# Moving the chunk inverses and the selection against each other in a two-block transformer kernel

## The reference

```python
# DeltaNet branch: a scan over chunks, after a triangular inverse for each chunk
lmat = jnp.where(strict, jnp.einsum('nbhid,nbhjd->nbhij', k_beta, kc) * decay, 0.0)
tmat = lax.linalg.triangular_solve(eye + lmat, eye, left_side=True, lower=True, unit_diagonal=True)
u = jnp.einsum('nbhij,nbhjd->nbhid', tmat, v_beta)
w = jnp.einsum('nbhij,nbhjd->nbhid', tmat, k_beta * jnp.exp(gc)[..., None])
# per chunk: v_new = u - w @ state ; o = q @ state + a @ v_new ; state = decay * state + k^T @ v_new

# Sparse attention branch: an index score picks the keys
dots = jnp.einsum('bqhd,bsd->bqhs', qi_b, ki)
score = jnp.einsum('bqh,bqhs->bqs', wi_b, jax.nn.relu(dots))
score = jnp.where(causal[None], score, -jnp.inf)
_, idx = lax.top_k(score, 128)      # for each block of 128 queries
```

## Time and profile before

| | us |
|---|---|
| median of 3 runs (1946.12 to 1949.91) | 1947.81 |
| the profiled execution's own time | 1946.41 |
| its span, first to last instruction | 1944.6 |
| TensorE busy | 1930.8 (99%) |
| VectorE busy | 1018.0 (52%) |
| ScalarE busy | 888.2 (46%) |
| GpSimd busy | 850.2 (44%) |

### The profile page before, as it was taken

How to read it: one execution, slowest core, us unless ns; L and a number is a source line. 1 busy time by engine, 2 the same in 40 slices (tenths; PEclk the granted TensorE clock), 3 DMA queues, 4 the chain that set the end, 5 groups by cost and what they waited for, 6 DMA issues and landing times.

```text
span 1944.6 us, 23731 instructions
## 1 busy us (share of the span) xinstructions
PE 1930.8 (99%) x9106; PEld 1532.8 (79%) x9106; DVE 1018.0 (52%) x1832; ACT 888.2 (46%) x1355; POOL 850.2 (44%) x644
## 2 busy tenths in 40 slices
PE   9999999999999999999999999999999999999999
PEld 6878887877788878787877888677766788888887
DVE  5757755555745668766464647575644436101210
ACT  6455553344345455543344355586555344312321
POOL 5545432433445454422434445455322445444443
PEclk9999999999999999999999999999999999999999
DMA  5334542423535235632414545322111332222232
GB/s 202 128 118 131 138 134 80 155 77 124 185 102 177 88 114 148 163 106 71 153 65 141 192 151 163 135 77 98 65 55 55 119 108 87 99 97 98 98 114 71
DMA packets 94575, 227.69 MB, mean 117 GB/s; under 512 B 29976, under 2 KB 33048, under 8 KB 93152
## 3 DMA queue, kind: packets, MB, share of 16 engines
q1 hardware_dynamic: 88768, 223.03, 35.1%
q10 hardware_dynamic: 5696, 3.15, 0.6%
HBM read 194.01 MB, written 24.64 MB: 112 GB/s over the span
## 4 chain that ended last, share of the span: by engine, by line
PE 86%; DVE 7%; DMA 2%; ACT 2%; SPq 1%; issue 1%; POOL 1%; ACTq 0%; DVEq 0%
PE bank L442 85%; DVE kv L376 1%; DVE ER L376 1%; PE bank L446 1%; SPq L371 1%; DMA X<-inverses 1%; DVE scs L401 1%; DMA kv<-blocks 1%; DVE tmp L376 1%; DVE m8s L398 0%; ACT lt L428 0%; DVE lt L386 0%; DVE tmp L386 0%; ACT wh L431 0%; DMA st<-units 0%
## 5 line engine op out<-in xcount | busy, mean ns | idle before, releaser
L376 POOL TENSOR_TENSOR wl<-st,wh 128x512 fp32r<-128x512 f32 x602 | 803.4, 1357 | 1020.2 <-ACT wh L431 1020.1
L442 PE MATMUL bank<-hh,wh 128*128 128x512 f32 x1616 | 651.2, 404 | 1.9 <-ACT hh L428 0.6
L442 PE MATMUL bank<-hh,wl 128*128 128x512 f32 x1616 | 629.2, 390 | 0.0
L442 PE MATMUL bank<-hl,wh 128*128 128x512 f32 x1616 | 628.8, 390 | 0.0
L431 ACT ACTIVATE wh<-st 128x1024 fp32r<-128x1024 f32 (+1 forms) x302 | 316.8, 1049 | 238.3 <-PE bank L442 190.5
L442 PEld LDWEIGHTS bank<-hh,wh 128*128 128x128 f32 x1616 | 303.3, 188 | 90.5 <-issue 26.0
L442 PEld LDWEIGHTS bank<-hl,wh 128*128 128x128 f32 x1616 | 303.6, 188 | 67.2 <-issue 6.9
L442 PEld LDWEIGHTS bank<-hh,wl 128*128 128x128 f32 x1616 | 303.3, 188 | 64.6
L376 DVE TENSOR_TENSOR xt<-xt,bank 128x512 f32<-128x512 f32 x40 | 27.4, 686 | 236.0 <-PE bank L442 236.0
L428 ACT ACTIVATE tmp<-bank 128x512 f32<-128x512 f32 x70 | 41.7, 596 | 158.2 <-PE bank L442 151.5
L442 PE MATMUL bank<-fh,wh 128*128 128x512 f32 x256 | 99.6, 389 | 0.0
(11 more groups left out here) (344 smaller groups left out, 2833.4 us busy)
## 6 DMA issues: line engine op xcount, KB each, us to landing
st<-units SPq DMA_DIRECT2D x300, 512.0 KB, 3.5
gates<-tmp SPq DMA_DIRECT2D x48, 256.0 KB, 2.7
gt<-gates SPq DMA_DIRECT2D x48, 256.0 KB, 3.6
pads<-tmp SPq DMA_DIRECT2D x32, 128.0 KB, 2.7
qk<-tmp SPq DMA_DIRECT2D x16, 256.0 KB, 4.2
x_scratch<-xt SPq DMA_DIRECT2D x2, 2048.0 KB, 8.7
xt<-x_scratch SPq DMA_DIRECT2D x2, 2048.0 KB, 8.2
ph<-phi SPq DMA_DIRECT2D x8, 512.0 KB, 4.7
```

The source lines that it names most:

```text
L376: return NOTHING if self.e is None else self.e.tensor_tensor(out, a, b, op)
L442: return NOTHING if self.e is None else self.e.matmul(out, lhsT, rhs, start=start, stop=stop, skip_group_check=share)
```

## The change

Five numbers at the top of the file, and the idle counts of ScalarE and SyncE that follow from them. `INVERSE` is how many steps TensorE passes between its last product for the chunk matrices and the first W product: 17 in place of 21. `BACK` is how many of these steps stand behind the inverses on VectorE. `CUTS` has five cuts in place of seven, so the inverses take six steps in place of eight; they begin at the same step as before. `SELECT` holds the idle steps ahead of the blocks b = 1, 2, 3 of the selection: (20, 1, 1) in place of (8, 12, 3), so block 1 starts 12 steps later, block 2 one step later and block 3 one step sooner. All engines follow it. GpSimd's instructions keep their order.

```diff
-INVERSE, BACK = 21, 11
+INVERSE, BACK = 17, 9
-CUTS = (4, 8, 11, 14, 17, 21, 25)
-SELECT = (8, 12, 3)
+CUTS = (4, 10, 15, 20, 25)
+SELECT = (20, 1, 1)
...
             # ScalarE, delta(l): ahead of the copy for the transposed inverses
-            yield from idle(INVERSE - BACK + 6)
+            yield from idle(INVERSE - BACK + 4)
...
             # ScalarE, delta(l): behind XT<-inverses_t
-            yield from idle(BACK - 8)
+            yield from idle(BACK - 6)
...
             # SyncE, delta(l): ahead of inverses<-kv
-            yield from idle(INVERSE - BACK + 2)
+            yield from idle(INVERSE - BACK + 3)
...
             # SyncE, delta(l): between inverses<-kv and X<-inverses
-            yield from idle(3)
+            yield from idle(2)
```

## The result

| | before | after |
|---|---|---|
| median of the runs | 1948.03 us (4 runs, 1946.12 to 1949.91) | 1976.76 us (4 runs, 1973.44 to 1979.10) |
| profiled execution, its span | 1946.4, 1944.6 | 1979.1, 1977.3 |
| mean granted clock of the profiled execution | 1.00 | 0.99 |

A forecast was written before the change was run, and what follows sets the result against it. The prediction took TensorE, busy 99% of the span, as the bound. Stall 22.6, clock 4, fetch 0 and recurrence 3 sum to 29.6 us, on 1946.4 giving 1976.0, written as 1977; range 1964 to 1983.

The forecast's parts named there:

- The stall: Block 1's second score pair: TensorE waits for banks 2 and 3 behind VectorE's inverses, 11.3 us a layer, 22.6 in all.
- The clock: Behind the stall on TensorE: a slow restart at a lower clock, 2 us a layer, 4 us in all.
- The fetch of the inverses: `X<-inverses` ahead of the W products: issue and use shift alike, wait stays 0 to 1 us, no change counted.
- third rival: Head transposes: VectorE stays late by 16 top-k rounds, a late swap costs 2 to 4 us a layer; 1982 to 1987; 0.07.
- The recurrence: End of the layer, recurrence four steps sooner, block 3's pairs adjacent: -1.8 + 0.9 + 2.0 + 0.5; 3 us in all.
- The sum: All terms over the whole kernel: 22.6 + 4 + 0 + 3 = 29.6 us slower, written as 1977 us.
- The first one: Block 1's second pair: VectorE's sums are done when TensorE arrives, so no stall; 1944 to 1949 us; chance 0.07.
- the sixteen rounds: Block 1's top-k rounds on VectorE: now lie where it stood idle, hidden by the main matmuls, at no counted cost.
- The second rival: Block 1's second pair: GpSimd mostly misses the inverses, stall only 2.8 to 6 us a layer; 1954 to 1964; chance 0.08.

The follow-up runs named there:

- experiment 3: Changed kernel with the four scores of block 1 in banks 4 to 7, all positions kept: 1956.59 us, ratio 1.0047.
- experiment 9: Changed kernel with GpSimd computing only 128 of 1024 columns of `wl` from the fourth weight unit on (output differs): 1948.01 us, ratio 0.9997.
- experiment 5: Changed kernel with 44 added matmuls of 128x512, result unused, on TensorE ahead of the second score pair of block 1: 1972.26 us, ratio 1.0132.
- experiment 7: Changed kernel with SELECT (24, 0, 0), block 1's scores four steps later still and block 2's where they were: 1966.24 us, ratio 1.0103.
- Experiment 1: Kernel before with the new SELECT (20, 1, 1) alone; INVERSE, BACK and CUTS as before: 1972.31 us, ratio 1.0131.
- experiment 8: Kernel of experiment 3 with SELECT (18, 1, 0), so a recurrence step also splits block 3's score pairs: 1952.19 us, ratio 1.0033.
- experiment 11: Kernel of experiment 8 with GpSimd computing only 128 of 1024 columns of `wl` from the fourth unit on: 1935.18 us, ratio 0.9937.
- experiment 4: Changed kernel with SELECT back at (8, 12, 3) and only VectorE's sixteen top-k rounds of block 1 behind the inverses: 1952.50 us, ratio 1.0033.
- experiment 12: Kernel before with GpSimd computing only 128 of 1024 columns of `wl` from the fourth weight unit on: 1940.70 us, ratio 0.9965.
- third series: The series of experiments 9 to 12, in which the kernel before has a median of 1947.37 us.
- experiment 10: Changed kernel with GpSimd's `wl` in eight instructions of 128 columns in place of two of 512, same work: 1984.14 us, ratio 1.0196.

## Why the prediction came out right, and where its terms did not

**The stall.** The place, the releaser and the cause were as predicted: the two banks, behind the inverses and a row of q. The size was 10.1 and 10.8 us, 20.9 for both, in place of 22.6. Both ends of that estimate were early, TensorE's by 0.9 us and VectorE's by 2.3, so the stall came out 1.4 us shorter in layer 0: TensorE arrived at 206.14 and not at 207.0; the inverses began at 178.83 and not at 181.1, and took 34.1 us to the end of the last one in place of 33.4, and the pair could start with the end of the first of the two sums, for bank 2, where the prediction waited for both. So it started at 216.2 and not at 218.5. Experiment 3 shows the cause by taking it away, experiment 9 shows what makes it that long: 9.2 us of losses to GpSimd. The prediction read 8.7 in the kernel before; of these the inverses' own instructions make 6.4 (26.7 us there, 20.3 in experiment 9), and the rest can only be rows of q and k that stood among them. What it made of it held: 2.8 us of stall without a meeting, where experiment 9 has 2.29 and 0.26, and more meetings once the rounds are gone. In experiment 3, where TensorE doesn't stand and GpSimd doesn't run dry, twelve instructions of `wl` meet them in place of ten, and they take 31.7 us, 11.4 of them lost.

**The clock.** Forecast 4 us for a slow restart behind the two stalls; experiment 5 makes it 3.9. The step that failed is that this was the only place. At the end of the recurrence the clock fell as well. The 24 main matmuls behind the scores of block 3 took 7.25 us in layer 0 and 7.85 in layer 1, in place of 5.67 in the kernel before, 3.8 us together. The eight score matmuls ahead of them took 5.54 in layer 1 and 4.59 in layer 0, 0.9 more. That is 4.7 us which no term had. The Trainium skill ("TensorE: Matmul & The Clock Gate", Part 1) has the clock at half after an idle stretch and back after sustained work. By that rule a stall is paid twice; the trace agrees for the long one. The runs show that a short wait can do it too, though not each time (experiments 3 and 7).

**The fetch of the inverses.** Forecast: no change, 0 to 1 us of wait. The wait of 1.4 us went, and not by the forecast's count: in layer 0 the fetch was issued 5.9 us ahead of the W products (237.54 and 243.44), where 8.4 had been reckoned, but its transfers landed within 3.7 us of their issue in place of 6.3 to 6.6. And the fetch has a neighbour that the prediction did not follow. Before, SyncE issued `pads<-tmp`, the swap of a row's halves, ahead of `X<-inverses` (235.38 and 236.86). Now it stands behind it. SyncE and VectorE in layer 1 of the changed kernel:

```profile
822.12 2.85 SPq L371 DMA_DIRECT2D X<-inverses  x4
...
826.31 1.13 SPq L371 DMA_DIRECT2D pads<-tmp  x2
```

```profile
833.36 0.75 DVE L386 SCALAR_TENSOR_TENSOR tmp<-tmp,col,tabs 128x512 f32<-128x512 f32 x1 [8.59 <-DMA pads<-tmp]
...
835.29 0.68 DVE L376 TENSOR_TENSOR lT<-bank,gcol 128x512 f32<-128x512 f32 x1
```

VectorE stood idle for 8.59 us until the swap had landed, did the row, and only then the `kv` and `lT` that TensorE was waiting for: 2.5 us in layer 1, 0.4 in layer 0. With the slow clock behind it (`XT,Y` 1.69 us in place of 0.87 in layer 0, the 12 main matmuls behind it 3.4 in place of 2.8) this is 2.9 + 1.4 = 4.3 us. It is the third rival's mechanism, a swap that comes late at the head transposes, at the low end of its price. VectorE's sixteen rounds, on which the rival put it, are not its cause: those ahead of the row had ended at 824.8. But the order of SyncE is not shown to be the whole of it either. The kernel before has the same idle time for a swap in layer 0:

```profile
242.07 1.64 DVE L386 SCALAR_TENSOR_TENSOR tmp<-tmp,col,tabs 128x512 f32<-128x512 f32 x1 [8.54 <-DMA pads<-tmp]
```

There `lT` was done at 249.75 and TensorE needed it at 251.52. The change asks for it five half tiles sooner and puts the swap behind the fetch, both at once. The swap took 4.4 to 6.5 us to land in layer 1 and 3.9 to 4.3 in layer 0, so its landing made a part of the difference between the layers. Experiment 1, without these edits, has no wait for `lT`, and experiment 9, with them but with little work on GpSimd, has none either. No run separates the two edits.

**The recurrence.** Forecast +3 us for both layers. One wait for `X` and one at the second pair of block 3 remained in each layer, as said; in waits it is 1.6 + 3.1 us after against 3.1 us before, so +1.6. But the whole can be read from start to start. From the row mean behind the stall to the first matmul of the next stage it takes 344.89 - 225.39 = 119.50 us in layer 0 and 934.15 - 810.05 = 124.10 in layer 1, before 333.08 - 213.36 = 119.72 and 904.02 - 784.07 = 119.95: 3.9 us more. Of these, 4.3 are the late swap, 0.9 the score pair at the low clock, and the fetch gave 1.4 back. That leaves +0.1 for the recurrence with its scores. The term was mis-sized by some 3 us; which of its four parts was too large, no trace separates.

**The sum.** 29.6 us forecast, 28.7 by the medians and 32.7 by the two profiled executions. The profiled one of the changed kernel is 2.3 us above its median. By the traces it is 20.9 for the stall, 3.9 for the clock behind it, 4.7 for the clock at the end of the layer, 4.3 for the swap, 0.1 for the recurrence, less 1.4 for the fetch: 32.5. (Some 1.1 us more around the moved pairs is offset by 1.0 us that this execution had gained ahead of any edit, by its first row mean of the stage at 131.38 in place of 132.37.) The stall and the recurrence were taken 4.6 us too large, the clock at the end of the layer and the swap, 9 us together, were missing, and the fetch gave 1.4 back. So the stall and its clock, three quarters of the sum, were understood. That the whole came within 1 us of the medians is luck: terms that were too large and terms that were missing offset each other in part, and what was left, 3 us, is about what these two executions lie apart from their medians (4.0 us in the difference).

**The rivals.** The first one said what the change would bring with no stall: 1944 to 1949. Experiments 3 and 8 have no stall at the banks and measure 1956.6 and 1952.2. In experiment 8 it is VectorE's backlog that meets the next product which TensorE needs; in experiment 3 the one execution traced, the fastest, shows the pair of block 3 and its clock, and the rest is open. Only with GpSimd's work cut down does the order of experiment 8 show a gain, experiment 11. So the sentence that the sixteen rounds "are hidden by the main matmuls" holds for an order and not in general. In the changed kernel VectorE had 6.5 us to spare behind the ten that stand ahead of the head products. In experiment 3, the same order without the stall, they just fitted (they ended at 233.37 in layer 0, and the row began at 233.51, with no wait of TensorE). With fourteen ahead, in experiment 8, they did not. No kernel with the full work was faster than the one before; the nearest are experiments 4 and 8, 6 us behind it. The second rival, a short stall, is what experiment 9 made by hand; with the full work it did not come.

## What to carry to other kernels

Count the backlog of the engine that is waited for over the whole stretch between two of its due times, not at one place. Here VectorE had to fit inverses, sixteen rounds and three rows into some 60 us, and each order of them that was tried moved the wait to another product: banks, an eviction on ScalarE, head products, or the end of the layer. Where the same order pays as soon as a second engine stops slowing the first, the thing to mend is that contention; none of the orders tried here made up for it. When a transfer moves in a queue, read what it has overtaken, and add the clock's restart to each long wait that becomes exposed, and allow for it, as a thing that may come or not, behind the short ones.

## What the runs showed of the hardware that was not expected

- A short wait may be followed by the low clock or not. A pause of 2.29 us between main matmuls of 512 columns (experiment 9, layer 0) left the granted clock at 1.00, while one of 1.44 us between two score matmuls that stand among main matmuls (experiment 7) was followed by 3.2 us at 0.50 in layer 0 and by none in layer 1. A wait of 1.56 us at the end of the recurrence, behind products of 128 columns, was followed by 3.4 us at 0.50 in layer 0 and 6.8 us in layer 1 of the changed kernel, and by none in layer 1 of experiment 3. Where TensorE was kept busy through 10 us of pause, the clock did not fall.
- Executions of one kernel differ by the clock where such waits are exposed: 11.8 us between the fastest and the slowest of experiment 3, but 0.9 and 1.5 us for experiments 11 and 12, whose clock stayed at 1.00. The clock is not all of it: the kernel before has 4.8 us between its fourteen executions of the third series, at 0.999 or 1.00.
- An instruction of GpSimd on 128x128 takes 508 ns in the mean of experiment 10, where one on 128x512 takes 1353 in the changed kernel; cut so, the same work took 41% longer, and each meeting cost VectorE 0.15 us in place of 1.0.
